# One-core decoder trunk on Trainium2: the expert stage's matmuls and weight loads in another order

## The reference, cut to what matters

```python
for l in range(DEPTH):                       # DEPTH = 2
    proj = rmsnorm(x, norm1_g[l]) @ w_in[l]
    ...                                      # MoBA, RWKV-7, SGU, differential attention
    x = x + mixed @ w_out[l]
    x = x + hier_moe(rmsnorm(x, norm2_g[l]), ...)
return rmsnorm(x, final_g)

def hier_moe(...):   # best of 4 groups, then best 2 of its 8 experts for each token
    ...
    def expert_block(args):
        xb, e = args
        hdn = jax.nn.silu(xb @ w_gate[e]) * (xb @ w_up[e])   # 1024 x 512 each
        return hdn @ w_down[e]                                # 512 x 1024
```

## Time and profile before

| | us |
|---|---|
| three runs: lowest, median, highest | 2200.77, 2209.47, 2238.36 |
| the profiled execution | 2196.54 |
| its span, first to last instruction | 2194.8 |
| TensorE matmuls busy | 1775.6 (81%) |
| VectorE busy | 588.1 (27%) |
| ScalarE busy | 323.2 (15%) |
| mean granted TensorE clock | 0.926 |
| moved by the DMA engines | 527.00 MB, 240 GB/s over the span |

### The profile page before, as it was taken

The page is one execution under the profiler, slowest core; times in us unless marked ns, Lnnn a source line. Parts: engine busy times, 40 slices in busy tenths (PEclk is TensorE's granted clock), DMA queues, the critical chain, the costliest instruction groups (busy, mean ns, idle before and its releaser), DMA issues. The chain is left out here.

```text
span 2194.8 us, 24263 instructions
## 1 busy us (share of the span) xinstructions
PE 1775.6 (81%) x9856; PEld 1056.3 (48%) x9856; DVE 588.1 (27%) x1169; ACT 323.2 (15%) x661; POOL 111.7 (5%) x133
## 2 busy tenths in 40 slices
PE   6799999997877867877379999998898777777761
PEld 3346677544544434444134566775554344444430
DVE  1162365533111111111124433565411111111113
ACT  1211233301000000000013123332100000000001
POOL 0010000001000000000100101000010000000001
PEclk9899999898999989989689999999999989998986
DMA  8911100026999999999441211002279999999993
GB/s 284 270 59 52 64 1 1 0 87 243 411 413 414 413 412 412 414 413 399 183 186 41 77 39 39 1 1 87 115 279 410 413 417 411 414 415 412 413 362 129
DMA packets 107428, 527.00 MB, mean 240 GB/s; under 512 B 35044, under 2 KB 35812, under 8 KB 88420
## 3 DMA queue, kind: packets, MB, share of 16 engines
q1 hardware_dynamic: 64740, 476.08, 53.6%
q0 software_dynamic: 38400, 33.79, 4.7%
q10 hardware_dynamic: 4224, 16.25, 3.1%
HBM read 481.83 MB, written 44.04 MB: 240 GB/s over the span
## 5 line engine op out<-in xcount | busy, mean ns | idle before, releaser
L702 PE MATMUL banks<-RING,TOK 128*64 128x256 f32 x4224 | 484.2, 385 | 82.5 <-DMA RING<-in_w_up 41.6
L702 PEld LDWEIGHTS banks<-RING,TOK 128*64 128x64 f32 x4224 | 320.9, 139 | 263.5 <-DMA RING<-in_w_up 56.5
L717 PE MATMUL banks<-RING,XS 128*64 128x512 f32 x1056 | 272.0, 661 | 42.7 <-issue 24.2
L438 PE MATMUL banks<-RING,XNT 128*128 128x512 f32 x512 | 224.1, 593 | 0.0
L717 PEld LDWEIGHTS banks<-RING,XS 128*64 128x64 f32 x1056 | 89.5, 153 | 185.5 <-issue 184.0
L930 ACT ACTIVATE XS<-banks 128x256 f32<-128x256 f32 x64 | 24.5, 383 | 990.3 <-PE banks L702 990.3
L1298 DVE TENSOR_TENSOR XS<-XS,banks 128x256 f32<-128x256 f32 x66 | 27.8, 421 | 505.3 <-PE banks L702 505.3
L438 PEld LDWEIGHTS banks<-RING,XNT 128*128 128x128 f32 x512 | 95.8, 190 | 113.1 <-issue 112.4
L695 PE MATMUL banks<-CF,TOK 128*128 128x128 f32 (+1 forms) x272 | 50.9, 346 | 111.3 <-DMA TOK<-x_slots 109.1
L429 PE MATMUL banks<-XNT,RING 128*128 128x512 f32 x256 | 110.4, 593 | 1.1 <-ACT XNT L787 1.1
L1319 DVE COPY XS<-banks 128x512 f32<-128x512 f32 x64 | 44.3, 691 | 250.0 <-PE banks L717 250.0
(11 more groups left out here) (249 smaller groups left out, 1735.1 us busy)
## 6 DMA issues: line engine op xcount, KB each, us to landing
RING<-in_w_gate SPq DMA_DIRECT2D x66, 2048.0 KB, 27.6
RING<-in_w_up SPq DMA_DIRECT2D x66, 2048.0 KB, 28.1
RING<-in_w_down SPq DMA_DIRECT2D x66, 2048.0 KB, 25.2
RING<-in_w_in_blocks SPq DMA_DIRECT2D x12, 2048.0 KB, 11.3
TOK<-x_slots SPq DMA_DIRECT2D x32, 512.0 KB, 23.8
y_slots<-XS POOLq DMA_DIRECT2D x64, 256.0 KB, 19.4
x_slots<-TOK ACTq DMA_DIRECT2D x11, 1024.0 KB, 32.7
RING<-in_w_out_blocks SPq DMA_DIRECT2D x4, 2048.0 KB, 7.7
```

Of the source, the lines that this page charges most:

```text
L438: last = mm(bank[:, :], XNT[:, k, i * P:(i + 1) * P], w[:, k, :], start=(k == 0), stop=(k == KD - 1))
L702: last = mm(bank[f * CAP:(f + 1) * CAP, 0:256], XT[:, k, h * CAP:(h + 1) * CAP], w[:, k, f * 256:(f + 1) * 256], start=(k == 0), stop=(k = ...
L717: last = mm(PS[5][n * CAP:(n + 1) * CAP, :], HT[:, j, f * CAP:(f + 1) * CAP], w[:, k, n * BN:(n + 1) * BN], start=(k == 0), stop=(k == KF ...
```

## The change

Each stream's expert loop is turned by one step. TensorE does gate and up matmuls of expert e + 1 ahead of the turn and the down matmuls of expert e. SyncE's loads go in the order in which TensorE now reads them: gate and up of the next expert in front of this one's down. ScalarE and VectorE follow, with new waits for `gated` and `hidden` where one expert's tile could be overwritten by the next. Ring, slots, sizes and the extra block are as they were.

```diff
@@ -344,9 +344,10 @@
                         sp.wait_ge(proj_ps, BLOCK_USED[n + 3])
                         sp.dma_start(SLOT[n], w_out[one, n].rearrange("a p n -> p (a n)")).then_inc(slot_full[n], 16)
 
-                    def load(e, h, waits):
-
-                        for m, v in enumerate((wg_v, wu_v, wd_v)):
+                    def load(e, h, waits, parts=(0, 1, 2)):
+
+                        for m in parts:
+                            v = (wg_v, wu_v, wd_v)[m]
                             s = (2 + 3 * h + m) % 6
                             sp.wait_ge(*waits[m])
                             src = v[bass.ds(layer * NE + e, 1)]
@@ -366,12 +367,22 @@
 
                     sp.wait_ge(rows_sent, 1)
                     load_rows(0)
-                    with sp.Fori(1, NE // 2) as i:
-                        sp.wait_ge(xt_ps, i)
-                        load_rows(i)
-                        for h in range(2):
-                            e = 2 * i + h
-                            load(e, h, [(gate_ps, e - 1), (up_ps, e - 1), (y2_ps, e - 1)])
+                    def load_next(e, h, parts):
+                        load(e, h, [(gate_ps, e - 1), (up_ps, e - 1), (y2_ps, e - 1)], parts)
+
+                    sp.wait_ge(xt_ps, 1)
+                    load_rows(1)
+                    load_next(2, 0, (0, 1))
+                    with sp.Fori(1, NE // 2 - 1) as i:
+                        load_next(2 * i + 1, 1, (0, 1))
+                        sp.wait_ge(xt_ps, i + 1)
+                        load_rows(i + 1)
+                        load_next(2 * i, 0, (2,))
+                        load_next(2 * i + 2, 0, (0, 1))
+                        load_next(2 * i + 1, 1, (2,))
+                    load_next(NE - 1, 1, (0, 1))
+                    load_next(NE - 2, 0, (2,))
+                    load_next(NE - 1, 1, (2,))
 
                     sp.wait_ge(routed, 3)
                     nov = sp.value_load(OVI[0:1, NOV:NOV + 1], min_val=0, max_val=NOV)
@@ -726,18 +737,27 @@
                         pe.wait_ge(slot_full[slot], 16 * (i + full0[slot] + 1))
                         return SLOT[slot]
 
-                    def expert(i, h, last=False):
+                    def gate_up(i, h, first=False):
 
                         e = 2 * i + h
                         if h == 0:
                             pe.wait_ge(xt_copied, i + 1)
+                        if not first:
+                            pe.wait_ge(gated, e)
                         gate_or_up(weights(0, i, h), PS[2], h).then_inc(gate_ps, 1)
+                        if not first:
+                            pe.wait_ge(hidden, e)
                         gate_or_up(weights(1, i, h), PS[3], h).then_inc(up_ps, 1)
-                        if h == 1 and not last:
-                            pe.wait_ge(rows_full, 16 * (i + 2))
-                            pe.sem_inc(pe_passed, 1)
-                            turn_rows(P, xt_ps)
+
+                    def rows_of(i):
+                        pe.wait_ge(rows_full, 16 * (i + 1))
+                        pe.sem_inc(pe_passed, 1)
+                        turn_rows(P, xt_ps)
+
+                    def hidden_down(i, h):
+                        e = 2 * i + h
                         pe.wait_ge(hidden, e + 1)
+                        pe.sem_inc(pe_passed, 1)
                         turn_hidden(ht_ps)
                         pe.wait_ge(y2_copied, e + 1)
                         pe.wait_ge(ht_copied, e + 1)
@@ -746,11 +766,16 @@
                     pe.wait_ge(route_in, 1)
                     pe.wait_ge(rows_full, 16)
                     turn_rows(P, xt_ps)
+                    gate_up(0, 0, first=True)
                     with pe.Fori(0, NE // 2 - 1) as i:
-                        for h in range(2):
-                            expert(i, h)
-                    expert(NE // 2 - 1, 0)
-                    expert(NE // 2 - 1, 1, last=True)
+                        gate_up(i, 1)
+                        rows_of(i + 1)
+                        hidden_down(i, 0)
+                        gate_up(i + 1, 0)
+                        hidden_down(i, 1)
+                    gate_up(NE // 2 - 1, 1)
+                    hidden_down(NE // 2 - 1, 0)
+                    hidden_down(NE // 2 - 1, 1)
                     nov = pe.value_load(OVI[0:1, NOV:NOV + 1], min_val=0, max_val=NOV)
                     with pe.If(nov > 0):
                         pe.wait_ge(y2_copied, NE + 1)
@@ -923,11 +948,17 @@
                     act.wait_ge(exp_in, 2)
                     ac(RW[:, 656:660], RW[:, 656:660], ACT.Exp).then_inc(exp_done, 1)
 
-                    with act.Fori(0, NE // 2) as i:
+                    def gate(e, first=False):
+                        act.wait_ge(gate_ps, e + 1)
+                        if not first:
+                            act.wait_ge(hidden, e)
+                        ac(HS, PS[2][:, 0:256], ACT.Silu).then_inc(gated, 1)
+
+                    gate(0, first=True)
+                    gate(1)
+                    with act.Fori(1, NE // 2) as i:
                         for h in range(2):
-                            e = 2 * i + h
-                            act.wait_ge(gate_ps, e + 1)
-                            ac(HS, PS[2][:, 0:256], ACT.Silu).then_inc(gated, 1)
+                            gate(2 * i + h)
                     nov = act.value_load(OVI[0:1, NOV:NOV + 1], min_val=0, max_val=NOV)
                     with act.If(nov > 0):
                         with act.Fori(0, nov) as j:
@@ -1303,28 +1334,33 @@
                     dve.wait_ge(xt_ps, 1)
                     copy_rows(P, xt_copied)
                     dve.sem_inc(y2_copied, 1)
-                    def expert(i, h, first=False, last=False):
-                        e = 2 * i + h
+                    def hide_expert(e):
                         dve.wait_ge(gated, e + 1)
                         dve.wait_ge(up_ps, e + 1)
                         hide(hidden)
+
+                    def expert(i, h, first=False, last=False):
+                        e = 2 * i + h
+                        if h == 0 and not last:
+                            dve.wait_ge(xt_ps, i + 2)
+                            copy_rows(P, xt_copied)
                         dve.wait_ge(ht_ps, e + 1)
                         copy_hidden(ht_copied)
-                        if h == 1 and not last:
-                            dve.wait_ge(xt_ps, i + 2)
-                            copy_rows(P, xt_copied)
+                        if h == 0 or not last:
+                            hide_expert(e + 1)
                         dve.wait_ge(y2_ps, e + 1)
                         if not first:
                             dve.wait_ge(y2_stored[h], 8 * NE * layer + 16 * i)
                         V.tensor_copy(YS[h], PS[5][:, :]).then_inc(y2_copied, 1)
 
+                    hide_expert(0)
                     for h in range(2):
                         expert(0, h, first=True)
                     with dve.Fori(1, NE // 2 - 1) as i:
                         for h in range(2):
                             expert(i, h)
-                    expert(NE // 2 - 1, 0)
-                    expert(NE // 2 - 1, 1, last=True)
+                    for h in range(2):
+                        expert(NE // 2 - 1, h, last=True)
                     nov = dve.value_load(OVI[0:1, NOV:NOV + 1], min_val=0, max_val=NOV)
                     with dve.If(nov > 0):
                         dve.wait_ge(y2_stored[0], 8 * NE * (layer + 1))
```

## The result

| | before | after |
|---|---|---|
| median of 20 runs | 2220.01 us | 2243.08 us |
| lowest, highest | 2196.66, 2275.61 | 2213.39, 2284.43 |
| ratio of undisturbed runs, 95% interval | | 1.0077 [1.0039, 1.0115] |
| profiled execution | 2196.54 | 2219.77 |
| mean granted TensorE clock | 0.926 | 0.936 |

The ratio compares only undisturbed runs, those within 1.5% of the fastest run of their kernel, while the medians take all 20. By the ratio the change costs 0.8%, some 17 us (9 to 26 of 2220). I had forecast 2208, from 2191 to 2226, and a loss of 5.2 us. The direction held; the time is outside the range.

The account below looks back on a forecast made before the run. Weight loads at 413 GB/s were taken to bound the expert stage, so loop terms were zero; the stage's end cost +2.6 us a layer, +5.2 in all, giving 2201.7 or 2214.7 by footing, 2208 taken halfway, range 2191 to 2226.

Parts of the forecast that it names:

- What bounds the kernel: Expert stage, mid-loop: weight loads at 413 GB/s and share 1.02 set the pace, 16.5 us an expert; TensorE needs 12.3.
- The loop's terms of zero: Expert loop and its start: removed wait gains 0; load order, new waits and start cost 0; row copy 0 to 4.2 us.
- steps 1 and 2: Stage end: down 30 starts at 1036.84, block's requests follow at 1041.6 to 1043.3, queue dry for at most 3 us.
- Steps 3 and 4: Block's loads: restart 0.5 us plus 0 to 1.6 lost, 15.9 us of bytes, 1.1 landing; -1.3 to +4.5 us a layer.
- dip: Slow stretch before the block's loads in the kernel before, 309 GB/s at share 1.08 from 1035 to 1045; 2.5 us.
- step 5: Stage end: expert 30's output store must land before the block's rows are copied; +2.6 us a layer, upper bound +7.5.
- two paths: Stage end: the block's loads, -1.3 to +4.5 us, and expert 30's store, +1.8 to +3.5 or up to +7.5.
- The footing: Whole kernel: base time to which the change's +5.2 us is added; 2208 taken halfway, 6.5 us either way.
- two anchors: Whole kernel: forecast sum of 2201.7 us on the profiled execution's footing and 2214.7 on the three-run median's.
- A: Stage end: dip goes and the store lands in about 10 us; -1.3 us a layer, 2200.2 us; chance 0.21.
- B: Expert loop: clock falls and TensorE becomes the bound; +115 us, 2323, at clock 0.65; chance 0.05.
- C: Expert loop: freed slots pace the loads, so TensorE's waits of 54.3 + 8.8 us a layer go; 2082 us; chance 0.04.

Follow-up runs that it names:

- e3: Kernel before, with the extra block's requests also waiting for the up matmuls of expert 31; stretch to the block's gate matmuls 522.2 and 522.1 us, ratio 1.0128.
- e4: Changed kernel's TensorE, ScalarE and VectorE, but loads in the order of the kernel before; median 2418 us, ratio 1.0959.
- e5: Kernel before, with the extra block's requests behind the down matmuls of expert 31; one execution, stretch to the block's gate matmuls 527.3 and 527.3 us.
- e6: Loads in the changed order, TensorE, ScalarE and VectorE as in the kernel before; stretch 529.9 and 527.8 us, ratio 1.0358.
- the early request: Changed kernel, but the block's rows, gate and up weights are requested after expert 30's gate and up matmuls; stretch 518.6 and 517.4 us, ratio 0.9984 to before.
- the split block: Kernel before, with a semaphore for each of the block's matrices and VectorE's wait for expert 30's store only ahead of its output copy; ratios 1.0053 and 0.9924.

## Why the prediction was wrong

**What bounds the kernel: right.** The loop is paced by bytes. The runs without the block give the sharpest form: 498.4 against 498.3 us.

**The loop's terms of zero: right** as a sum (498.4 against 498.3, 499.2 against 499.7); the runs do not part the wait removed, the waits added, the copy of rows and the start. What I had not seen is that SyncE's half is needed for it: alone, the new order on TensorE, ScalarE and VectorE costs 105 us a layer.

**The end, steps 1 and 2: right.** Down 30 starts at 493.5 (forecast 493.9), the request leaves at 498.3 (498.7 to 500.4), and the queue stands dry for two microseconds (at most 3), behind four in which the engines run out one by one.

**Steps 3 and 4: the term that was mis-sized.** I had 17.5 us from request to gate matmuls, 21.6 at most with restart and dip, and measured 24.5; the five kernels with a late request (`e3`, `e4`, `e5`, `e6` and the changed one) have 24.0 to 24.6. Bytes start no sooner than 1.2 us behind the request, not 0.5; 1.3 us are lost in restarting (233 GB/s for 3 us), as reckoned. The fixed cost of 2.0 us that I took from the Trainium skill, "DMA: Bandwidth & Descriptors", section "Anatomy of one DMA", is given there for the path of GpSimd's transfers, while these loads are SyncE's; nor would it have moved my sum, whose +2.6 came from step 5. What was missing is the end: I divided 6.55 MB by the rate of sixteen engines, and the stores of experts 30 and 31, which now run beside these very loads, leave four engines with five microseconds more to do. Taking those stores away takes 4 to 6 us away. A landing is the landing of the slowest engine. The sign of it stood in my own rows. From 1059 to 1060 the share was 0.25 at 91 GB/s; I read that as all engines done by 1059.3 and 1.1 us to land, but some of them worked on:

```profile
1059.75:1060.00 0.25, 0.00 (x0) 0.00 (x0) 0.00 (x0) 0.00 (x0) 0.00 (x0) 0.50 0.10 33
```

So before, too, a few engines finished last, by about one microsecond instead of five.

**Step 5: right in size, wrong in its role.** The store of 30 took 20 us (issued 1054.12, VectorE's copy at 1074.15), forecast 19.3, but it does not decide; the weights do, 4 us later. The forecast of +2.6 us a layer became +5.1 and +6.2, within the bounds of -1.3 and +7.5. But those were the bounds of two paths together: +2.6 was read from this step, which does not decide, and the path that does decide came out at +5.3, above its own upper bound of +4.5. So the sign held partly by luck, since it was taken from the path that does not decide.

**The footing: the largest part of the miss.** I reckoned from a profiled execution of 2196.54 and three runs, halfway between two anchors. My 2208 is 2203 for the kernel before and 5.2 for the change. Over 20 runs the kernel before has a median of 2220.01, so the footing was 17 us low before any change. By itself that would give 2225, just inside the range; with the 6 us by which I had the stage's loss too small it is 2231, outside. The measured median of the changed kernel is another 12 us above, with a scatter of 71 us from lowest to highest, and no stretch of the changed kernel's own explains those 12. The range of 35 us was narrower than the scatter of one kernel, 42 us over my own four numbers and 79 over 20.

**The rivals.** A (the end is covered) fell, but half of it is true: the dip does not occur ahead of down 31 in the changed kernel, which lands 2.9 us earlier. B (the clock falls) went the other way, 0.92 to 0.97. The new waits are longer than the 1.4 us that I set against B, up to 4.3, but shorter than the 7.6 of before. The Trainium skill's page "TensorE: Matmul & The Clock Gate", section "HAM oscillation", has bursts that are shorter than the wait for the next weights start at the lower clock each time; the two traces agree in direction, and no run tried it by itself. It was worth no time here: the DMA engines moved 413 GB/s at either clock. C (waits count) fell: those waits went, and others took their place.

## What to carry to other kernels

Where a stage is bound by its loads, look for the places where the queue of loads can run dry, above all its end, and what each request waits for; making an engine that waits anyway wait less brings nothing, and it can push a later request behind the last load. A request should wait for the matmuls that free its own slot, not for those that free the last of three, and a consumer for the one matrix it needs. When the order on the compute side is turned, the loads must be turned with it, since one queue serves its waits in order.

## What the runs showed of the hardware

**The mixers' length varies from execution to execution.** The same instructions took 531 to 573 us in the first layer and 535 to 583 in the second, over all the profiles of this study. The profiles show the granted clock with it: 0.91 and 0.82 in 300 to 400 of the kernel before and of the early request, and 0.93 and 0.74 in the like stretch of the second layer of the kernel before and of the late request:

```profile
300.00:400.00 100.00, 95.25 (x601) 76.42 (x599) 52.36 (x133) 33.09 (x96) 0.00 (x0) 0.91 0.00 1
```

```profile
300.00:400.00 100.00, 95.25 (x545) 75.48 (x545) 47.12 (x116) 29.87 (x85) 0.00 (x0) 0.82 0.00 1
```

```profile
1400.00:1500.00 100.00, 95.44 (x583) 74.26 (x583) 53.98 (x140) 34.32 (x102) 0.00 (x0) 0.93 0.00 1
```

```profile
1402.00:1502.00 100.00, 96.19 (x483) 73.50 (x484) 42.38 (x112) 27.32 (x82) 0.00 (x0) 0.74 0.00 1
```

TensorE is as busy, 95 to 96 us of 100, at a lower clock and with fewer instructions done. Why the clock differs the runs don't show. An effect of 1% drowns in that: the split block measured 1.0053 and 0.9924 on two occasions, with intervals that exclude 1 on opposite sides, while its stage was 15 to 16 us shorter both times. The medians of all runs agree better, 2226.57 against 2232.62 and 2218.31 against 2224.23, 0.3% below before both times. So these intervals do not hold all of the uncertainty, and the ratios of 1.0077 and 1.0055 for the changed kernel are to be read with that in mind. The stage's length repeats far better: 533.1 to 534.1 us in the four stages of the changed kernel, and within 2.6 us in every kernel that was profiled twice.

**A loop's first pass taken out moved a table load.** ScalarE's busy time in mid-stage fell from 29.08 us to 11.14. The kernel before loads an activation table once in each pair of experts, 1.28 us, 32 times in all, the changed one twice in all, whose first two silus of a layer stand ahead of the loop. From the kernel before:

```profile
638.61 0.38 ACT L930 ACTIVATE XS<-banks 128x256 f32<-128x256 f32 x1 [13.03 <-PE banks L702]
639.01 1.28 ACT L930 ACT_TABLE_LOAD   x1
```

It lay beside the up matmuls, and the loop was no longer for it (498.4 against 498.3 us). That the first passes taken out of the loop are the reason was not tried by itself.
